# The opening in another order with transfers held back, and the recurrence's norm with low parts by GpSimd and its last sums in PSUM

## The chip, the cores and the metric

The kernel runs on one core of one Trainium2 chip. The metric is the device time of one execution in microseconds (us), the median of the runs. Engines: TensorE (PE in the rows, PEld its weight loads), VectorE (DVE), ScalarE (ACT), GpSimd (POOL), SyncE (SP), whose queue issues all transfers.

## The reference

Two transformer-like blocks over 512 tokens of width 1024, in float32. What bears on the change:

```python
def first_block(x, mem, ...):
    n = rmsnorm(h, norm_mix_pre)
    proj = n @ w_in                     # pool input, q k v, memory queries xq, gates
    y_pool = pool_mixer(p_in, w_pool_mix, pool_scale) @ w_pool_o   # trailing means over 2, 4, 8, 16 tokens
    y_sb = stick_breaking_attention(q, k, v) @ w_sb_o
    mem_n = rmsnorm(mem, norm_mem)      # 256 memory tokens
    y_x = memory_cross_attention(xq, mem_n, w_mem_kv) @ w_x_o      # 4 heads, softmax over 256
    ...
    ff = (silu(gu[..., :D_FF]) * gu[..., D_FF:]) @ w_ffn_out
    h = h + rmsnorm(ff, norm_ffn_post)

def second_block(x, ...):
    h = _rmsnorm(x, norm_mix[0])
    q, f, i, g = split(h @ hgrn_w_in, 4)
    o = chunk_gated_recurrence(silu(q), 1 - forget, i, log(forget))  # 8 heads of 128
    ...                                 # feed-forward, latent attention, feed-forward
```

## The kernel before

**Layout.** Activations lie feature by feature: a tile is 128 features by 512 tokens, eight tiles (KD = 8) make the residual; the memory's tiles are 128 by 256. Matrix products are float32 in three parts: weight and operand are each split into a high part (ScalarE copies them into a float32r buffer) and a low part (value less high part), and `products` (L220) issues high x high, low x high and high x low, lines 226 to 228. A norm's gain is applied with the high and low parts of its input (L426 or L1200 on ScalarE, L309 or L1240 on VectorE); its 1/rms is applied to the product's output (`dve_scaled`, L367), so the products of a norm start before its sum of squares is known.

**Weights.** All weights pass through one stream of units: a unit is eight 128 x 128 blocks (512 KB), and there are four slots (SLOTS). SyncE loads unit u into slot u % 4 once the low part of unit u - 4 is done (`s_lo`); ScalarE makes its high part (`high`, L201) once TensorE has used unit u - 4; GpSimd makes its low part in two halves of 512 columns (L2709, L2710), except units 0 to 6 and two later ones, which VectorE does (L465, L1275). `high_to(u)` places ScalarE's high parts in its program. Every engine runs its own program in order; the order is written out by hand, and an engine waits at a semaphore with everything behind it.

**Opening** (`act_start`, `dve_start`, `pe_memory`). Units 0 to 3 are the memory's keys and values: TensorE multiplies each with the eight memory tiles, 24 matmuls of 256 columns a unit. ScalarE's order is: high part of unit 0, memory tiles 0 to 3, unit 1, memory tiles 4 to 7, units 2 to 4, input tiles 0 and 1, unit 5, input tiles 2 and 3, unit 6, squares of the memory, input tiles 4 to 7, their squares. VectorE's order follows it. SyncE's order is: first gains, unit 0, the memory in two halves, units 1 to 3, input tiles 0 and 1, unit 4, tiles 2 and 3, units 5 and 6, tiles 4 to 7, the remaining parameters (1.6 MB), positions, unit 7. Then `pe_norm_start` takes units 4 to 6 together (WIDE = 3): for each of the eight input tiles nine matmuls of 512 columns.

**Memory values and cross-attention** (`pe_memory_values`, `pe_cross`, `dve_cross`). The values are transposed in two steps of two transposes, both through the same bank, each followed by a copy by ScalarE (L508). Then, for each of four token blocks tb: scores of four heads (L591), VectorE's maxima (L702), ScalarE's exponentials (L664), VectorE's probabilities (L713), and TensorE's transposes of them (L612). TensorE puts a weight tile of 24 matmuls (the next pool group or the first stick query) between scores and transposes; VectorE works on a pool group (`dve_pool`: copies L565, shifted sums L566, L569, L572) between the probabilities of one block and the maxima of the next.

**Recurrence's norm** (`dve_last_kept`, `act_post_norm`, `dve_post_norm`, stage "hgrn"). Before it VectorE finishes the feed-forward's output and its squares' sum in two halves of the tokens (L1157), each followed by a sum over partitions on TensorE and rstd on ScalarE; the low part of the norm's third unit stands between the two half sums. Then per tile j: VectorE scales and adds to the residual (L1217, L1220), ScalarE makes the high part (L1200), VectorE the low part (L1240), TensorE nine matmuls. Tile 0 goes in two halves. The squares go through two buffers, VectorE adds the seven sums at the end (L324), and TensorE forms the total over partitions (L280, one float32 matmul, which stands as two instructions in the trace) in the middle of the tile g of the first head. After the total come ScalarE's rstd (L285, L287) and the first head's chain.

## Time and profile before

| | |
|---|---|
| three runs, median | 2038.65 us (2036.48 to 2039.67) |
| the profiled execution, time | 2039.15 us |
| its span, first to last instruction | 2037.3 us |
| instructions | 26328 |
| VectorE, ScalarE, GpSimd busy | 47%, 45%, 42% |
| chain that ended last, TensorE's share | 91% |
| mean granted TensorE clock | 0.994 |

The span is 1.85 us shorter than the execution's own time; the rest lies outside the first and last instruction. In the views a row gives the start (us from the span's start), the duration, engine, line, operation, output and inputs, and in brackets how long the engine had been idle before and who released it. The duration of a matmul reaches over its pipeline; the pace of a row of matmuls is read from their starts.

### The profile page before, as it was taken

What the parts mean: (1) busy time and instruction counts of PE and PEld (TensorE: products, weight loads), DVE (VectorE), ACT (ScalarE), POOL (GpSimd) and SP (SyncE); (2) the same over time, 40 slices, a digit from 0 to 9 for tenths busy, and PEclk for the clock granted to TensorE, in tenths of its full rate; (3) what the DMA queues carried; (4) which work ended last, traced back from release to release, by engine and by line L of the source; (5) the groups of instructions that cost most, each with busy time, mean ns of one, the idle gap of its engine ahead of it and who ended that gap; (6) DMA issues with size and microseconds to landing.
All of it is one profiled execution on the core that took longest, in us unless ns stands there. A gap on an engine that the chain in (4) does not pass through costs nothing.

```text
span 2037.3 us, 26328 instructions
## 1 busy us (share of the span) xinstructions
PE 1996.1 (98%) x10819; PEld 1616.2 (79%) x10819; DVE 956.6 (47%) x1475; ACT 924.6 (45%) x1286; POOL 851.4 (42%) x668
## 2 busy tenths in 40 slices
PE   7999999999999998899999999999999999999999
PEld 6788888878888887677777888888876778888887
DVE  5744433254301315888885453155155555521551
ACT  6566554343313324665665443244266545432441
POOL 1243344535544552333435444444431254444442
PEclk9999999999999999899999999999999999999999
DMA  6122222223322322121212232232210222332321
GB/s 246 52 91 75 73 83 83 90 76 106 101 93 97 100 94 72 53 74 64 74 64 83 93 104 93 84 113 93 88 47 26 79 85 91 104 102 84 103 96 71
DMA packets 51672, 178.30 MB, mean 88 GB/s; under 512 B 5728, under 2 KB 8928, under 8 KB 51424
## 3 DMA queue, kind: packets, MB, share of 16 engines
...
q14 instruction: 34, 0.28, 0.0%
...
## 4 chain that ended last, share of the span: by engine, by line
PE 91%; DVE 5%; ACT 2%; issue 1%; POOL 1%; DMA 0%; SPq 0%; ACTq 0%; DVEq 0%; POOLq 0%
PE ps_gemm L226 24%; PE ps_gemm L228 23%; PE ps_gemm L227 23%; PE ps_attend L226 4%; PE ps_attend L227 4%; PE ps_attend L228 4%; PE ps_attend L1671 1%; PE ps_attend L838 1%; PE ps_attend L2457 1%; PE ps_attend L2523 1%; PE ps_attend L2458 1%; PE ps_attend L280 1%; ACT weights_high L201 1%; PE ps_gemm L1651 1%; PE ps_attend L1700 0%
## 5 line engine op out<-in xcount | busy, mean ns | idle before, releaser
L2709 POOL TENSOR_TENSOR weights_low<-weights_raw,weights_high 128x512 fp32r<-128x512 f32 (+1 forms) x332 | 426.0, 1283 | 1164.5 <-ACT weights_high L201 1164.1
L226 PE MATMUL ps_gemm<-normed_high,weights_high 128*128 128x512 f32 x1665 | 663.3, 398 | 6.0 <-DVE normed_low L1240 2.8
L228 PE MATMUL ps_gemm<-normed_low,weights_high 128*128 128x512 f32 x1665 | 648.5, 390 | 0.0
L227 PE MATMUL ps_gemm<-normed_high,weights_low 128*128 128x512 f32 x1665 | 648.3, 389 | 0.0
L201 ACT ACTIVATE weights_high<-weights_raw 128x1024 fp32r<-128x1024 f32 (+1 forms) x341 | 340.7, 1006 | 450.3 <-PE ps_attend L228 218.8
L2710 POOL TENSOR_TENSOR weights_low<-weights_raw,weights_high 128x512 fp32r<-128x512 f32 (+1 forms) x332 | 440.7, 1327 | 0.0
L226 PEld LDWEIGHTS ps_gemm<-normed_high,weights_high 128*128 128x128 f32 x1665 | 314.0, 189 | 79.3 <-issue 8.6
L227 PEld LDWEIGHTS ps_gemm<-normed_high,weights_low 128*128 128x128 f32 x1665 | 314.3, 189 | 65.2 <-issue 3.6
L228 PEld LDWEIGHTS ps_gemm<-normed_low,weights_high 128*128 128x128 f32 x1665 | 313.8, 188 | 65.7
L226 PE MATMUL ps_gemm<-operands_high_low,weights_high 128*128 128x512 f32 (+1 forms) x552 | 216.1, 391 | 0.9 <-POOL weights_low L2710 0.5
L228 PE MATMUL ps_gemm<-operands_high_low,weights_high 128*128 128x512 f32 (+1 forms) x552 | 214.2, 388 | 0.0
L227 PE MATMUL ps_gemm<-operands_high_low,weights_low 128*128 128x512 f32 (+1 forms) x552 | 214.1, 388 | 0.0
L367 DVE TENSOR_TENSOR scratch<-ps_gemm,rstd 128x512 f32<-128x512 f32 x89 | 60.8, 688 | 217.4 <-PE ps_gemm L228 200.5
L367 DVE TENSOR_TENSOR squares<-ps_gemm,rstd 128x512 f32<-128x512 f32 x106 | 73.0, 689 | 161.9 <-PE ps_gemm L228 130.1
L1401 ACT ACTIVATE ps_attend<-squares,parameters 128x512 f32<-128x512 f32 x88 | 68.9, 783 | 170.2 <-DVE squares L367 170.1
L226 PE MATMUL ps_attend<-operands_high_low,weights_high 128*128 128x512 f32 (+1 forms) x336 | 128.8, 383 | 10.3 <-DVE operands_high_low L309 10.2
L227 PE MATMUL ps_attend<-operands_high_low,weights_low 128*128 128x512 f32 (+1 forms) x336 | 127.8, 380 | 0.0
L228 PE MATMUL ps_attend<-operands_high_low,weights_high 128*128 128x512 f32 (+1 forms) x336 | 127.7, 380 | 0.0
L226 PEld LDWEIGHTS ps_gemm<-operands_high_low,weights_high 128*128 128x128 f32 x552 | 103.7, 188 | 23.0 <-issue 1.6
L228 PEld LDWEIGHTS ps_gemm<-operands_high_low,weights_high 128*128 128x128 f32 x552 | 103.6, 188 | 21.4
L227 PEld LDWEIGHTS ps_gemm<-operands_high_low,weights_low 128*128 128x128 f32 x552 | 103.7, 188 | 21.0 <-issue 0.2
L1461 DVE SCALAR_TENSOR_TENSOR ps_attend<-squares,parameters,ps_attend 128x511 f32<-128x511 f32 x88 | 66.4, 755 | 76.0 <-ACT ps_attend L1401 76.0
...
## 6 DMA issues: line engine op xcount, KB each, us to landing
...
```

The lines of the kernel that those rows point to most:

```text
L201: s.op.activation(m.wh[:, j * UNIT:j * UNIT + w], m.raw[:, j * UNIT:j * UNIT + w], ACT.Copy).then_inc(m.s_hi, 1)
L226: t.op.matmul(out, m.wh[:, c:c + P], xh, start=start and n == 0, stop=False, skip_group_check=True)
L227: t.op.matmul(out, m.wl[:, c:c + P], xh, start=False, stop=False, skip_group_check=True)
L228: ins = t.op.matmul(out, m.wh[:, c:c + P], xl, start=False, stop=stop and n == len(pairs) - 1, skip_group_check=True)
L280: t.op.matmul(out, m.col("ones", 0, P), src, start=True, stop=True).then_inc(*m.T.mark(*event))
L367: return v.op.tensor_tensor(dst, ps, m.rstd[:, 0:dst.shape[1]], ALU.mult)
L838: ins = t.op.matmul(zb[:, o:o + S - j * P], neg_tri if j == kb else neg_ones, x[:, ZOFF[j]:ZOFF[j] + S - j * P], start=False, stop=False, ...
L1401: s.op.activation(y, m.sq_tile(half), ACT.Identity, bias=m.col(f"conv_b{n - 1}", c), scale=m.col(f"conv_w{n - 1}", 88 + c)).then_inc(*m.A. ...
L1461: v.op.scalar_tensor_tensor(out=y[:, 1:S], in0=u[:, 0:S - 1], scalar=w(1), in1=y[:, 1:S], op0=ALU.mult, op1=ALU.add).then_inc(*m.V.mark(st ...
L1651: ins = t.op.matmul(bank[:, (c + 1) * P:(c + 1) * P + b - a], x.vtok[:, c * P:(c + 1) * P], x.cross[:, a:b], start=False, stop=c == 2, ski ...
L2709: g.op.tensor_tensor(m.wl[:, a], m.raw[:, a], m.wh[:, a].bitcast(F32), ALU.subtract)
L2710: g.op.tensor_tensor(m.wl[:, b], m.raw[:, b], m.wh[:, b].bitcast(F32), ALU.subtract).then_inc(m.s_lo, 1)
```

## The change

It has four parts.
- Opening. Unit 0's high and low parts are made in two halves, with memory tile 0 between them; all memory tiles come before unit 1; units 5 and 6 stand together. The memory is transferred in three parts (tiles 0 and 1, 2 and 3, 4 to 7). SyncE waits for unit 0 to have landed before it issues unit 2. Input tiles 2 and 3 go out behind unit 6, 4 and 5 behind unit 7, 6 and 7 behind unit 8; the remaining parameters and the positions behind unit 9.
- Memory values and cross-attention. The four transposes of the values go out together, with one copy. Half a weight tile stands ahead of the first scores, and each further half ahead of the next scores; VectorE's maxima stand inside the pool group, after its first sum; the low part of one pool group moves.
- The second half sum ahead of the recurrence is placed before the low part of a unit.
- Recurrence's norm. For tiles 4 to 7 ScalarE makes a scaled float32 copy beside the high part, and GpSimd subtracts, before its low part of the norm's fourth unit. ScalarE squares every tile right behind its high part, each into a place of its own. VectorE adds five of the sums; TensorE adds the squares of tiles 6 and 7 in PSUM in the sum over partitions, straight behind the norm.

```diff
--- before.py
+++ after.py
@@ -247,6 +249,9 @@
+GPSIMD_LOWS, VECTOR_SUMS = 4, 5
...
 def pieces(stage):
@@ -330,19 +335,42 @@
+def low_done(m, stage, j, half):
...
+    return (m.G if stage == "hgrn" and j >= GPSIMD_LOWS else m.V).at(*piece_event(stage, "low", j, half))
...
 def pe_norm_start(m, t, stage, events):
...
     for kb, half in pieces(stage):
-        t.wait_ge(*m.V.at(*piece_event(stage, "low", kb, half)))
+        t.wait_ge(*low_done(m, stage, kb, half))
...
             pe_memory_total(m, t)
-    if stage not in ("ffn0", "hgrn"):
+    if stage == "hgrn":
+        pe_total_of_squares(m, t, stage)
+    elif stage != "ffn0":
         pe_norm_total(m, t, stage)
...
+def square_place(m, j):
...
+    return (m.ss[:, :], m.sq_tile(1), m.sq_tile(0))[j] if j < 3 else m.big_tile(j)
...
+def pe_total_of_squares(m, t, stage):
...
+    for j in range(VECTOR_SUMS + 1, KD):
+        t.wait_ge(*m.A.at(stage, "square", j))
+        t.op.matmul(m.ab(3), m.col("ones", 0, P), square_place(m, j), start=j == VECTOR_SUMS + 1, stop=False,
+                    skip_group_check=True)
+    t.wait_ge(*m.V.at(stage, "sum", VECTOR_SUMS))
+    t.op.matmul(m.ab(3), m.col("ones", 0, P), m.ss[:, :], start=False, stop=True, skip_group_check=True)\
+        .then_inc(*m.T.mark(stage, "total"))
 def pe_norm_total(m, t, stage):
@@ -378,6 +406,13 @@
+MEMORY_PARTS = ((0, 2), (2, 4), (4, 8))
+def memory_part(j):
+    return [a <= j < b for a, b in MEMORY_PARTS].index(True)
@@ -387,8 +422,12 @@
 def pe_memory(m, t):
...
     for j in range(4):
-        base = take_unit(m, t)
+        base = take_unit(m, t) if j else 0
         for kb in range(KD):
+            if j == 0:
+                t.wait_ge(*m.V.at("first", "low"))
+                if kb == KD // 2:
+                    take_unit(m, t)
@@ -422,7 +461,7 @@
             (src, hi, _), gain = start_tile(m, stage, j)
-            s.wait_ge(*((m.s_x[j // 2], 16) if stage == "in" else (m.s_mem[j // 4], 16)))
+            s.wait_ge(*((m.s_x[j // 2], 16) if stage == "in" else (m.s_mem[memory_part(j)], 16)))
@@ -433,16 +472,21 @@
     s.tables(LOGEXP)
-    high_to(m, s, 0)
-    s.wait_ge(m.s_gains, 16)
-    highs("mem", range(4))
-    high_to(m, s, 1)
-    highs("mem", range(4, KD))
+    s.wait_ge(m.s_raw[0], 16)
+    for half in range(2):
+        sl = slice(half * UNIT // 2, (half + 1) * UNIT // 2)
+        ins = s.op.activation(m.wh[:, sl], m.raw[:, sl], ACT.Copy)
+        if half == 0:
+            ins.then_inc(*m.A.mark("first", "high"))
+            s.wait_ge(m.s_gains, 16)
+            highs("mem", range(1))
+    ins.then_inc(m.s_hi, 1)
+    s.unit += 1
+    highs("mem", range(1, KD))
...
     highs("in", (0, 1))
-    high_to(m, s, 5)
+    high_to(m, s, 6)
     highs("in", (2, 3))
-    high_to(m, s, 6)
@@ -472,15 +516,18 @@
-    weights((0,))
-    lows("mem", range(4))
-    weights((1,))
-    lows("mem", range(4, KD))
-    weights((2, 3, 4))
+    sl = slice(0, UNIT // 2)
+    v.wait_ge(*m.A.at("first", "high"))
+    v.op.tensor_tensor(m.wl[:, sl], m.raw[:, sl], m.wh[:, sl].bitcast(F32), ALU.subtract).then_inc(*m.V.mark("first", "low"))
+    lows("mem", range(1))
+    sl = slice(UNIT // 2, UNIT)
+    v.wait_ge(m.s_hi, 1)
+    v.op.tensor_tensor(m.wl[:, sl], m.raw[:, sl], m.wh[:, sl].bitcast(F32), ALU.subtract).then_inc(m.s_lo, 1)
+    lows("mem", range(1, KD))
+    weights((1, 2, 3, 4))
     lows("in", (0, 1))
-    weights((5,))
+    weights((5, 6))
     lows("in", (2, 3))
-    weights((6,))
@@ -495,17 +542,13 @@
 def pe_memory_values(m, t):
-    for j in range(2):
-        t.wait_ge(*m.V.at("mem", "kv", 2 + j))
-        if j:
-            t.wait_ge(*m.A.at("mem", "values", j - 1))
-        pe_to_tokens(m, t, ("mem", "values", j), m.ab(2), m.big[:, (2 + j) * M:(3 + j) * M], 2)
+    t.wait_ge(*m.V.at("mem", "kv", 3))
+    pe_to_tokens(m, t, ("mem", "values"), m.ab(2), m.big[:, 2 * M:4 * M], 4)
 def act_memory_values(m, s):
-    for j in range(2):
-        s.wait_ge(*m.T.at("mem", "values", j))
-        s.op.activation(m.big[:, (4 + j) * M:(5 + j) * M], m.ab(2, M), ACT.Copy).then_inc(*m.A.mark("mem", "values", j))
+    s.wait_ge(*m.T.at("mem", "values"))
+    s.op.activation(m.big[:, 4 * M:6 * M], m.ab(2), ACT.Copy).then_inc(*m.A.mark("mem", "values"))
@@ -549,7 +592,7 @@
-def dve_pool(m, v, g):
+def dve_pool(m, v, g, between):
@@ -564,6 +607,8 @@
         v.op.tensor_tensor(dst[:, w:S], src[:, w:S], src[:, 0:S - w], ALU.add).then_inc(*m.V.mark("pool", "sum", g, k))
+        if k == 0:
+            between()
@@ -580,9 +625,15 @@
 def pe_cross(m, t):
     keys, vals, xq, prob, pt = cross_tiles(m)
-    t.wait_ge(m.s_par, 16)
-    t.wait_ge(*m.V.at("cross", "q", 1))
-    t.wait_ge(*m.V.at("mem", "kv", 3))
+    def tile(tb, half):
+        bank = pool_bank(tb + 1)
+        if half == 0 and bank < 2:
+            t.wait_ge(*m.V.at("cross", "q", bank))
+        if half == 0 and tb == TB - 1:
+            t.wait_ge(*m.A.at("pool", "scaled", 0))
+        event = ("pool", tb + 1) if tb < TB - 1 else ("stick", "q", 0)
+        pe_tile(m, t, event, m.gb(bank), m.nh, m.nl, (2 * half, 2 * half + 1))
@@ -592,27 +643,26 @@
+    tile(0, 0)
+    t.wait_ge(m.s_par, 16)
+    t.wait_ge(*m.V.at("cross", "q", 1))
...
     for tb in range(TB):
-        bank = pool_bank(tb + 1)
-        if bank < 2:
-            t.wait_ge(*m.V.at("cross", "q", bank))
-        if tb == TB - 1:
-            t.wait_ge(*m.A.at("pool", "scaled", 0))
-        event = ("pool", tb + 1) if tb < TB - 1 else ("stick", "q", 0)
-        pe_tile(m, t, event, m.gb(bank), m.nh, m.nl, (0, 1))
+        tile(tb, 1)
...
             pe_pool(m, t, tb - 1)
-        pe_tile(m, t, event, m.gb(bank), m.nh, m.nl, (2, 3))
         if tb < TB - 1:
+            tile(tb + 1, 0)
             scores(tb + 1)
+        else:
+            t.wait_ge(*m.A.at("pool", "scaled", 1))
+            pe_tile(m, t, ("stick", "k", 0), m.gb(3), m.nh, m.nl, (0,))
         t.wait_ge(*m.V.at("cross", "prob", tb))
-        t.wait_ge(*(m.A.at("cross", "pt", tb - 1) if tb else m.A.at("mem", "values", 1)))
+        t.wait_ge(*(m.A.at("cross", "pt", tb - 1) if tb else m.A.at("mem", "values")))
...
         ins.then_inc(*m.T.mark("cross", "pt", tb))
-    t.wait_ge(*m.A.at("pool", "scaled", 1))
-    pe_tile(m, t, ("stick", "k", 0), m.gb(3), m.nh, m.nl, (0, 1))
+    pe_tile(m, t, ("stick", "k", 0), m.gb(3), m.nh, m.nl, (1,))
@@ -698,6 +748,8 @@
     def maxima(tb):
+        if tb == TB:
+            return
@@ -713,10 +765,10 @@
         ins.then_inc(*m.V.mark("cross", "prob", tb))
-        dve_pool(m, v, tb)
-        if tb < TB - 1:
-            maxima(tb + 1)
-        if tb:
+        if tb == TB - 1:
+            dve_pool_low(m, v, TB - 3)
+        dve_pool(m, v, tb, lambda: maxima(tb + 1))
+        if tb and tb != TB - 2:
@@ -1201,12 +1253,18 @@
             act_half_rstd(m, s, before, 1)
-        if half != (0,) and j < 3:
+        if stage == "hgrn" and j >= GPSIMD_LOWS:
+            s.op.activation(scaled_tile(m, j), src, ACT.Identity, scale=m.col(gain, j))\
+                .then_inc(*m.A.mark(stage, "scaled", j))
+        if stage == "hgrn" and half != (0,):
+            s.op.activation(square_place(m, j), src, ACT.Square).then_inc(*m.A.mark(stage, "square", j))
+        elif half != (0,) and j < 3:
...
             high_to(m, s, late)
-    for j in range(3, KD):
-        act_square(m, s, stage, j, residual_tile(m, j)[0])
+    if stage == "ffn0":
+        for j in range(3, KD):
+            act_square(m, s, stage, j, residual_tile(m, j)[0])
 def dve_branch(m, v, before, stage, j, half, post_gain):
@@ -1235,6 +1293,8 @@
     def low(j, half):
+        if stage == "hgrn" and j >= GPSIMD_LOWS:
+            return
@@ -1254,8 +1314,15 @@
         dve_unit_low(m, v, fourth_unit(m, stage))
-    for j in range(1, KD):
-        dve_square_sum(m, v, stage, j)
+    if stage == "hgrn":
+        for j in range(1, VECTOR_SUMS + 1):
+            v.wait_ge(*m.A.at(stage, "square", j))
+            if j > 1:
+                v.wait_ge(*m.V.at(stage, "sum", j - 1))
+            v.op.tensor_tensor(m.ss[:, :], m.ss[:, :], square_place(m, j), ALU.add).then_inc(*m.V.mark(stage, "sum", j))
+    else:
+        for j in range(1, KD):
+            dve_square_sum(m, v, stage, j)
 def fourth_unit(m, stage):
@@ -1502,8 +1569,8 @@
             dve_half_sum(m, v, "ffn0out", 0)
+    dve_half_sum(m, v, "ffn0out", 1)
     dve_unit_low(m, v, fourth_unit(m, "hgrn") - 1)
-    dve_half_sum(m, v, "ffn0out", 1)
 def pe_post_ffn(m, t):
@@ -1726,9 +1793,7 @@
     else:
-        g_tile((0, 1))
-        pe_norm_total(m, t, "hgrn")
-        g_tile((2, 3))
+        g_tile(range(4))
@@ -2695,6 +2760,19 @@
+def scaled_tile(m, j):
...
+    return m.big_tile(4 + j)
...
+def gpsimd_lows(m, g, stage):
...
+    for j in range(GPSIMD_LOWS, KD):
+        _, hi, lo = residual_tile(m, j)
+        g.wait_ge(*m.A.at(stage, "scaled", j))
+        g.op.tensor_tensor(lo, scaled_tile(m, j), hi.bitcast(F32), ALU.subtract).then_inc(*m.G.mark(stage, "low", j))
...
 def gpsimd_program(m, g):
@@ -2703,6 +2781,8 @@
             continue
+        if u == fourth_unit(m, "hgrn"):
+            gpsimd_lows(m, g, "hgrn")
@@ -2711,7 +2791,7 @@
-INPUT_BEHIND = {3: (0,), 4: (1,), 6: (2, 3)}
+INPUT_BEHIND = {3: (0,), 6: (1,), 7: (2,), 8: (3,)}
 def sync_program(m, q):
@@ -2723,16 +2803,18 @@
             q.wait_ge(m.s_lo, u - SLOTS + 1)
+        elif u == 2:
+            q.wait_ge(m.s_raw[0], 16)
...
         if u == 0:
-            for k in range(2):
-                sl = slice(k * 4 * M, (k + 1) * 4 * M)
+            for k, (a, b) in enumerate(MEMORY_PARTS):
+                sl = slice(a * M, b * M)
...
                 q.op.dma_start(m.h[:, sl], m.dram_x[:, sl]).then_inc(m.s_x[k], 16)
-        if u == SLOTS + WIDE - 1:
+        if u == SLOTS + WIDE + 2:
```

## Rows read from the trace of the kernel before

**Rows 1.** Page, section 1: busy time and share of the span, TensorE to GpSimd

```profile
PE 1996.1 (98%) x10819; PEld 1616.2 (79%) x10819; DVE 956.6 (47%) x1475; ACT 924.6 (45%) x1286; POOL 851.4 (42%) x668
```

**Rows 2.** Waits, TensorE, whole span: engine line, released by, us in total, times, longest

```profile
PE ps_attend L226 <- DVE operands_high_low L309: 10.2, 2, 8.2
...
PE ps_gemm L1648 <- DVE scratch L1948: 3.6, 1, 3.6
...
PE ps_gemm L280 <- DVE sum_of_squares L1157: 2.8, 2, 1.6
```

**Rows 3.** Timeline of TensorE in the opening (columns as told above)

```profile
8.16 0.55 PE L226 MATMUL ps_attend<-operands_high_low,weights_high 128*128 128x256 f32 x1 [8.16 <-DVE operands_high_low L309]
...
13.10 0.58 PE L226 MATMUL ps_attend<-operands_high_low,weights_high 128*128 128x256 f32 x1 [2.04 <-DVE operands_high_low L309]
...
17.01 0.28 PE L226 MATMUL ps_attend<-operands_high_low,weights_high 128*128 128x256 f32 x1
...
24.92 0.40 PE L226 MATMUL ps_gemm<-normed_high,weights_high 128*128 128x512 f32 x1
```

**Rows 4.** Timeline of ScalarE and VectorE in the opening

```profile
4.57 1.06 ACT L201 ACTIVATE weights_high<-weights_raw 128x1024 fp32r<-128x1024 f32 x1 [2.56 <-DMA weights_raw<-weights_full]
...
6.99 1.71 ACT L426 ACTIVATE operands_high_low<-scratch,parameters 128x256 fp32r<-128x256 f32 x4 [1.36 <-DMA scratch<-memory_tiles]
...
7.53 1.68 DVE L309 SCALAR_TENSOR_TENSOR operands_high_low<-scratch,parameters,operands_high_low 128x256 fp32r<-128x256 f32 x4 [0.65 <-ACT operands_high_low L426]
...
10.34 1.06 ACT L201 ACTIVATE weights_high<-weights_raw 128x1024 fp32r<-128x1024 f32 x1 [1.64 <-DMA weights_raw<-weights_full]
...
23.40 1.23 DVE L465 TENSOR_TENSOR weights_low<-weights_raw,weights_high 128x1024 fp32r<-128x1024 f32 x1 [0.33 <-ACT weights_high L201]
```

**Rows 5.** Windows (busy us by engine, clock, DMA share, GB/s); landing of weights_raw, 0 to 60

```profile
10.00:20.00 10.00, 7.96 (x48) 7.67 (x48) 7.63 (x10) 7.41 (x11) 0.00 (x0) 1.00 0.95 369
...
48.00:50.00 2.00, 2.00 (x7) 1.51 (x6) 1.75 (x2) 0.00 (x0) 2.00 (x2) 0.50 0.66 190
...
DMA to landing us min/median/max: 3.2/7.7/11.8
```

**Rows 6.** Timeline of TensorE from the memory's values to the kept product

```profile
46.48 0.41 PE L374 MATMUL ps_attend<-parameters,scratch 128*128 128x128 f32 x2 [3.47 <-ACT scratch L508]
...
48.69 0.63 PE L227 MATMUL ps_gemm<-normed_high,weights_low 128*128 128x512 f32 x1
...
91.70 1.02 PE L531 MATMUL ps_gemm<-sum_of_squares,parameters 128*128 128x512 f32 x2
```

**Rows 7.** Timeline of VectorE at the end of cross-attention

```profile
83.80 1.14 DVE L565 COPY sum_of_squares<-squares 128x2 f32<-128x2 f32 x1
...
90.47 1.28 DVE L723 TENSOR_TENSOR operands_high_low<-ps_attend,operands_high_low 128x512 fp32r<-128x512 f32 x2
```

**Rows 8.** Timeline of TensorE at the recurrence's norm

```profile
798.99 0.55 PE L226 MATMUL ps_gemm<-normed_high,weights_high 128*128 128x256 f32 x1 [2.43 <-issue]
...
807.78 0.50 PE L226 MATMUL ps_gemm<-normed_high,weights_high 128*128 128x512 f32 x1 [0.62 <-DVE normed_low L1240]
...
820.93 1.02 PE L280 MATMUL ps_attend<-sum_of_squares,parameters 128*128 128x512 f32 x2
```

**Rows 9.** Timeline of GpSimd, ScalarE and VectorE at the recurrence's norm and behind it

```profile
805.89 1.29 POOL L2710 TENSOR_TENSOR weights_low<-weights_raw,weights_high 128x512 fp32r<-128x512 f32 x1
...
806.08 1.65 DVE L1240 SCALAR_TENSOR_TENSOR normed_low<-residual,parameters,normed_high 128x512 fp32r<-128x512 f32 x1
...
806.20 0.72 ACT L1200 ACTIVATE normed_high<-residual,parameters 128x512 fp32r<-128x512 f32 x1 [1.30 <-DVE residual L1220]
...
814.69 5.39 DVE L324 TENSOR_TENSOR sum_of_squares<-sum_of_squares,squares 128x512 f32<-128x512 f32 x7
...
823.38 1.89 DVE L367 TENSOR_TENSOR scratch<-ps_gemm,rstd 128x512 f32<-128x512 f32 x3 [3.30 <-ACT rstd L287]
...
836.23 3.60 POOL L2709 TENSOR_TENSOR weights_low<-weights_raw,weights_high 128x512 fp32r<-128x512 f32 x1 [9.31 <-ACT weights_high L201]
```

6 lines of the change are left out of this document (4 added, 2 removed).

## The prediction

> **What bounds the kernel now.** I read the page first: TensorE is busy 98% of the span [rows 1], so a wait is worth removing only where TensorE itself stands still. The waits of TensorE over the whole span [rows 2] therefore come next. They are few, and they lie in the three places that the diff touches: the opening (10.2 us until the memory's low parts), the memory's values (3.5 us), and the start of the recurrence (3.6 us, and 2.8 us at the two half totals ahead of it). Last I read the timelines of those three places. What to see in them:
>
> Opening. TensorE starts at 8.16, stops after 12 matmuls, and starts again at 13.10 [rows 3]. The cause is one line up in ScalarE's list: memory tiles 4 to 7 stand behind the high part of the second unit, which waited for its transfer until 10.34 [rows 4]. From 13.10 to 17.01 there are 18 matmuls of 256 columns (0.22 us each, the lower clock level), from 17.01 to 24.92 there are 66 (0.12 us each, the upper level). The 96 matmuls of the memory product need 11.5 us at the upper level and now end at 24.92. The DMA engines move 369 GB/s in the stretch 10 to 20, with a share of 0.95, so transfers are a second limit close by [rows 5].
>
> Memory values. TensorE waits 3.47 us for a copy by ScalarE; behind it the granted clock is 0.50 of full, 1.2 GHz [rows 5], and six 512-column matmuls go at 0.43 us instead of 0.23 (one of them in [rows 6]).
>
> Recurrence. From the norm's total on the chain is ScalarE's rstd, then VectorE from 823.38, and it ends in TensorE's wait for VectorE of 3.6 us [rows 2, 9]. TensorE is not the bound there; the time of rstd is.
>
> The sum is made against the profiled execution, span 2037.3 and time 2039.15; the median of the three runs is 0.5 us below that.
>
> **Part 1, the opening.** Unit 0 is split in two, and only one memory tile stands between its halves. Unit 0 still lands at about 4.5: fewer transfers are outstanding, but the bytes ahead of it are the same. A half high part is half of 1.06, 0.55 us; a tile's high part is 1.71/4 = 0.43; a half low part 0.6, a tile's low part 0.42 [rows 4]. So: half high 5.1, half low 5.75, tile high 5.6, tile low 6.2. TensorE starts at 6.3 to 6.8 instead of 8.16. Tiles 1 to 7 follow at 0.42 us each on VectorE (6.9 to 10.1), faster than TensorE's six half-pace matmuls per two tiles (0.64 us a tile), so unit 0 ends near 11.4. The second unit is no longer ahead of tiles 4 to 7: high part 9.7 to 10.75, low part until 12.0 (1.23 [rows 4]). If the clock is up by then, three units at 2.88 us end at 20.7. Then the first norm needs unit 6. Its transfer goes out when unit 2's low part is done (13.2), behind unit 5. Bytes issued up to and with unit 6 are 5.4 MB; at 369 GB/s from 2 on [rows 5] they are in at 16.7 when served in order, but transfers share the engines, and the median landing in this stretch is 7.7 us after issue [rows 5]: 17 to 21, I take 19. High part 1.05 and low part 1.23 put the start of the norm at 21.2. Gain 24.92 - 21.2 = 3.7 us. Ends: 5 us if nothing is late and the clock rises by 10; 1.5 us if unit 6 takes the longest landing seen (11.8 us, to 25, is excluded only by its having less behind it, so I take 21.5 plus high, low and a TensorE still at the low level for 2 us). The inputs x (now behind units 3, 6, 7, 8) I cost at nothing: the first pair keeps its place, and tiles 4 to 7 are wanted only after eight microseconds of norm matmuls. The late parameters and positions go out three units later, about 17.5 to 19.5 instead of 16.7; they are wanted past 40, so that is free, and they leave the DMA to units 7 to 9.
>
> **Part 2, values and cross-attention.** The two copies become one, and half a tile (12 matmuls, 2.73 us) is put ahead of the scores, so the copy and the scaled queries are hidden. On today's clock: the first two transposes end at 43.0 (46.48 less the wait), the other two 0.3 later, the half tile at 46.0 and the scores (1.06) at 47.1, all at the upper level. That removes 3.5 us of waiting and 1.2 + 0.2 us of slow matmuls. From there VectorE decides. Its reduction of the scores is now placed after the first sum of each pool group, in order, so what is queued behind it (the rest of the pool group, then the next probabilities) waits for TensorE, where the scores come half a tile later. Played through with today's durations VectorE waits about 1.8 and 1.3 us there, and ends the fourth pool group at 86.3 and the attention's low parts at 88.3; those low parts today start at 90.47 and end 91.75 [rows 7]. TensorE starts the kept product, which needs them, at 88.4 instead of 92.6 [rows 6]. Gain 4.2; I take 3.7 because small VectorE copies that meet a GpSimd low part take 1.14 us instead of 0.15 [rows 7], and which of them meet one I can't tell. Ends 1.5 and 5.
>
> **Part 3, the recurrence's norm.** (a) The second half sum goes ahead of VectorE's low part of a unit (1.23 us): total and rstd of the second half come 0.9 us earlier, the first half's branch 0.7 us later, TensorE starts at 798.2 instead of 798.99 [rows 8]: 0.8 us. The wait of 0.62 before 807.78 [rows 8] goes with it: it is VectorE's low part of 1.65 us, which met GpSimd's [rows 9]. (b) VectorE drops four low parts of 0.7 us and two of seven sums (5.39/7 = 0.77 each [rows 9]); its sums begin at 814.7 - 2.6 (the lows) - 0.9 (the stall) - 0.5 (the earlier rstd) = 810.7. ScalarE has three passes per tile in place of two, each at most the 0.72 of a high part [rows 9], about 2.0 us, against TensorE's nine matmuls at 0.228, 2.06 us. GpSimd's low of 512 columns is 1.29 [rows 9]. The three are matched; the last low part comes at 814.5, so the norm ends at about 816.8 instead of 818.2 (820.93 less half a tile, 2.73). (c) TensorE gets three float32 sums in place of one: each is a pair of instructions and 0.86 us, +1.72 us, ahead of the total. (d) The low part of the unit after the norm is queued behind GpSimd's four: until 818.6. It is wanted at 820, so it is covered by a hair; uncovered it would cost 1 to 2 us of TensorE, which has room there. (e) VectorE's five sums, each with both operands in SBUF, now run beside GpSimd's last two lows and two weight halves. The row of 806.08 shows VectorE waiting for GpSimd's end [rows 9]; alternating, four of the sums wait 1.3 us each, and the fifth ends at 810.7 + 5 x 0.7 + 4 x 1.3 = 819.4. So the total is done at 820.2 against 821.8 (820.93 + 0.86 [rows 8]): 1.6 us. Without (e) TensorE alone would set it, 816.8 + 3 x 0.86 = 819.4, a gain of 2.4.
>
> The Trainium skill (SBUF — State Buffer, section "Who interferes with whom") states the rule that speaks against this part: a VectorE instruction with two SBUF inputs and a GpSimd instruction that reads SBUF exclude each other, whichever starts first. The row of 1.65 us agrees; without that rule part 3 would be 2.4, by it 1.6.
>
> rstd moves VectorE's chain (823.38) by the same amount, and TensorE's own work behind it (two tiles, 10.9 us) still fits. I take 1.6, ends 0 and 3.
>
> **Sum.** 3.7 + 3.7 + 1.6 = 9.0 us; 2039.15 - 9.0 = 2030.1, which I leave at 2030.0 against the median. Between these places TensorE waits for nobody longer than about a microsecond [rows 2], so what one of them gives is not taken back in the next.
>
> **Rivals.**
> 1. Only TensorE's side moves, VectorE's does not: in cross-attention its in-order wait for the later scores costs 2.7 us three times, less the 1.5 us it no longer waits; part 2 gives about 1.5 and unit 6 is late, part 1 gives 2: total 5 with part 3, 2034.3. For it: 0.95 DMA share, and VectorE at the end of that stage just in time. Against it: VectorE has some 7 us of waiting in that stage to absorb it.
> 2. The change doesn't do what it says in the opening: transfers share the engines so evenly that holding back unit 2 changes nothing, TensorE again stops before unit 1, and stays at the low level. Part 1 then gives 0.5 and the rest 5.3: 2033.4; with part 2 at its low end as well, 2036.
> 3. Slower: the exclusion of (e), at its dearest. One GpSimd half took 3.60 us at 836.23 [rows 9]. If each of VectorE's five sums waits for such a one, the fifth ends at 810.7 + 5 x (0.7 + 3.6) = 832, rstd is 11 us late, and TensorE, out of work, falls to the lower level for another 1.5 us: 2039.15 - 7.4 + 11 + 1.5 = 2044.2. Part 3 turns into a loss from a GpSimd instruction of 1.7 us on, and the whole kernel is slower from about 3 us on. Against it: the usual one is 1.3, and only six are near.
> 4. All goes through: 5 + 5 + 3, 2026.
>
> **How the numbers follow.** Forecast and its surroundings (2027.5 to 2032.5) 0.60; rival 4: 0.10; rivals 1 and 2 (2032.5 to 2036.5) 0.24; rival 3: 0.06 (not all of it past the bound). Range 2026.0 to 2035.5, which leaves 0.03 below and about 0.13 above. A measurement of this kernel tells 0.2%, 4.1 us, from no change: faster is below 2034.6, so 0.83; same 0.12; slower 0.05.
>
> **What would show it.** Right: the first norm matmul near 21 and no stop of TensorE before it longer than 1 us; no wait at the values' transposes and 512-column matmuls at 0.23 us behind them; the kept product about 8 us earlier than today; VectorE's last sum near 819 less 7.4, with sums of 2 us where GpSimd is busy; TensorE's wait for VectorE after the first head still about 3.5. Wrong: unit 6's transfer landing past 22, VectorE idle over 5 us for scores, or TensorE waiting for GpSimd's lows for more than 1 us in the norm.

## The result, and the profile after

The changed kernel takes 2026.64 us (median of 4 runs, 2025.69 to 2027.85) against 2038.91 (4 runs, 2036.48 to 2039.67): ratio 0.9938, 95% interval 0.9926 to 0.9950, a gain of 12.3 us where 9.0 was forecast. The two profiled executions differ by 12.5 us in span (2037.3 and 2024.8). Read at the same events, 11.8 us of the gain arise in the three places and nothing between them, and 0.7 us behind the last of them:

| event | before, us | after, us | lead | gained in the stretch |
|---|---|---|---|---|
| first TensorE matmul | 8.16 | 7.11 | 1.05 | 1.05 |
| first matmul of the first norm | 24.92 | 21.66 | 3.26 | 2.21 |
| fourth pool product (cross-attention) | 91.70 | 82.66 | 9.04 | 5.78 |
| last half tile of the feed-forward's branch | 791.89 | 782.92 | 8.97 | -0.07 |
| first matmul of the recurrence's norm | 798.99 | 789.03 | 9.96 | 0.99 |
| VectorE starts behind rstd | 823.38 | 811.55 | 11.83 | 1.87 |
| end of the span | 2037.3 | 2024.8 | 12.5 | 0.7 |

TensorE's waits over the whole span after the change (engine, line, released by; total, times, longest) answer to [rows 2]:

```profile
PE ps_attend L228 <- DVE operands_high_low L314: 7.1, 1, 7.1
PE ps_gemm L228 <- DVE normed_low L1300: 4.7, 4, 2.5
PE ps_attend L1738 <- DVE squares L2001: 2.5, 1, 2.5
PE ps_gemm L1715 <- DVE scratch L2013: 2.2, 1, 2.2
PE ps_gemm L285 <- DVE sum_of_squares L1209: 2.2, 2, 1.6
...
PE ps_gemm L228 <- POOL weights_low L2790: 1.0, 3, 0.5
```

The wait at the values is gone, the opening has one start in place of two, and GpSimd's low parts of the norm appear nowhere as a releaser. TensorE in the opening, to be read against [rows 3] (the row of 21.34 is the last of the memory's 96 matmuls):

```profile
7.11 0.55 PE L228 MATMUL ps_attend<-operands_high_low,weights_high 128*128 128x256 f32 x1 [7.11 <-DVE operands_high_low L314]
...
11.45 0.28 PE L228 MATMUL ps_attend<-operands_high_low,weights_high 128*128 128x256 f32 x1
...
12.76 0.36 PE L228 MATMUL ps_attend<-operands_high_low,weights_high 128*128 128x256 f32 x1 [0.43 <-DVE weights_low L509]
...
21.34 0.28 PE L230 MATMUL ps_attend<-operands_high_low,weights_high 128*128 128x256 f32 x1
...
21.66 0.47 PE L228 MATMUL ps_gemm<-normed_high,weights_high 128*128 128x512 f32 x1
```

From the start to 11.3 the pace is 0.21 us a matmul, from 11.45 on 0.12. I read this as the lower level (1.2 GHz) and the upper (2.4 GHz). The views' own figure for the granted clock reads 1.00 in both stretches, so in the opening the level is known from the pace alone; it is the same halving as that of the 512-column matmuls, 0.43 against 0.23 us, where the views do show 0.50 (48 to 50 in [rows 5]). Before, the slow pace lasted until 16.9 with a stop of 2.04 us inside. ScalarE and VectorE feed it:

```profile
4.68 0.63 ACT L478 ACTIVATE weights_high<-weights_raw 128x512 fp32r<-128x512 f32 x1 [2.67 <-DMA weights_raw<-weights_full]
5.94 0.51 ACT L465 ACTIVATE operands_high_low<-scratch,parameters 128x256 fp32r<-128x256 f32 x1 [0.63 <-DMA scratch<-memory_tiles]
...
10.31 1.99 ACT L203 ACTIVATE weights_high<-weights_raw 128x1024 fp32r<-128x1024 f32 x2
...
19.19 1.06 ACT L203 ACTIVATE weights_high<-weights_raw 128x1024 fp32r<-128x1024 f32 x1 [0.93 <-DMA weights_raw<-weights_full]
```

```profile
20.28 1.23 DVE L509 TENSOR_TENSOR weights_low<-weights_raw,weights_high 128x1024 fp32r<-128x1024 f32 x1 [0.48 <-ACT weights_high L203]
```

Unit 6 is there at 19.2 and its low part ends at 21.51; the norm starts 0.15 us behind that. TensorE's own row of matmuls ends at 21.46 (the last start and 0.12 us of pace). So two limits now meet within 0.05 us, the transfer of unit 6 and TensorE's 96 matmuls: an earlier transfer alone would give at most 0.2 us. In cross-attention, TensorE in the changed kernel (busy time of TensorE, its weight loads, VectorE, ScalarE and GpSimd, then granted clock, DMA share and GB/s), and below it the second wait of the kernel before, which [rows 2] doesn't show:

```profile
22.00:82.00 60.00, 59.87 (x284) 44.40 (x283) 45.39 (x90) 36.63 (x80) 22.68 (x16) 1.00 0.35 131
```

```profile
PE ps_attend L612 <- DVE scratch L713: 0.8, 1, 0.8
```

TensorE waits nowhere in this stage after the change, apart from 0.13 us at 71.44, and the granted clock stays at 1.00. Before, it waited 3.5 and 0.8 us, and for 3.4 us (47.6 to 51.0) the clock stood at 0.50, which costs half of that, 1.7 us. Together that is 6.0 us, and the stretch is 5.8 shorter: 61.0 us is TensorE's own work, and TensorE is the limit of the stage. VectorE there:

```profile
50.60 1.23 DVE L754 TENSOR_REDUCE small<-ps_attend 128x4 f32<-128x1024 f32 x1
...
59.09 1.23 DVE L754 TENSOR_REDUCE small<-ps_attend 128x4 f32<-128x1024 f32 x1 [1.30 <-PE ps_attend L642]
60.34 0.17 DVE L757 TENSOR_SCALAR small<-small 128x4 f32<-128x4 f32 x1
60.42 0.16 DVE L608 COPY sum_of_squares<-squares 128x2 f32<-128x2 f32 x1
...
74.99 1.15 DVE L608 COPY sum_of_squares<-squares 128x2 f32<-128x2 f32 x1
...
81.68 1.28 DVE L775 TENSOR_TENSOR operands_high_low<-ps_attend,operands_high_low 128x512 fp32r<-128x512 f32 x2
```

Inside the pool groups VectorE waits for the scores 1.3 us twice (59.09 and 67.57), and not at all the first time. The copy of two columns takes 0.16 us at 60.42 and 1.15 at 74.99, where it meets a GpSimd low part (74.37 to 76.11). The attention's low parts end at 82.96, 0.16 us before the first matmul of the kept product (83.12), so VectorE is close to being the limit but isn't. In the recurrence's norm, VectorE, GpSimd and TensorE:

```profile
800.96 2.39 DVE L1322 TENSOR_TENSOR sum_of_squares<-sum_of_squares,squares 128x512 f32<-128x512 f32 x2
803.46 4.99 DVE L1322 TENSOR_TENSOR sum_of_squares<-sum_of_squares,scratch 128x512 f32<-128x512 f32 x3
811.55 1.89 DVE L395 TENSOR_TENSOR scratch<-ps_gemm,rstd 128x512 f32<-128x512 f32 x3 [3.11 <-ACT rstd L292]
```

```profile
803.21 1.30 POOL L2773 TENSOR_TENSOR normed_low<-scratch,normed_high 128x512 fp32r<-128x512 f32 x1 [0.41 <-ACT scratch L1257]
804.47 1.73 POOL L2789 TENSOR_TENSOR weights_low<-weights_raw,weights_high 128x512 fp32r<-128x512 f32 x1
806.16 1.73 POOL L2790 TENSOR_TENSOR weights_low<-weights_raw,weights_high 128x512 fp32r<-128x512 f32 x1
```

```profile
789.03 0.55 PE L228 MATMUL ps_gemm<-normed_high,weights_high 128*128 128x256 f32 x1 [2.46 <-DVE normed_low L1300]
...
807.39 1.88 PE L369 MATMUL ps_attend<-scratch,parameters 128*128 128x512 f32 x4
809.11 1.02 PE L372 MATMUL ps_attend<-sum_of_squares,parameters 128*128 128x512 f32 x2
...
846.28 1.13 PE L1715 MATMUL ps_gemm<-scratch 128*128 128x128 f32 x8 [2.23 <-DVE scratch L2013]
```

VectorE's fifth sum ends at 808.5, 0.7 us before TensorE asks for it: TensorE goes from the norm through its three float32 sums without a wait.

### The profile page after: what moved, and what is told of

Read it like the earlier page. It is cut to its first block, busy times and chain, and to the rows that moved or that the text cites. A ratio compares the mean times of both kernels' runs of the same rounds, so it can differ in the third digit from the quotient of the medians.

```text
span 2024.8 us, 26338 instructions
## 1 busy us (share of the span) xinstructions
PE 1992.9 (98%) x10823; PEld 1613.2 (80%) x10823; DVE 953.5 (47%) x1470; ACT 927.1 (46%) x1290; POOL 859.0 (42%) x672
## 4 chain that ended last, share of the span: by engine, by line
PE 93%; DVE 4%; ACT 2%; issue 1%; POOL 1%; DMA 0%; SPq 0%; DVEq 0%; ACTq 0%; POOLq 0%
PE ps_gemm L228 24%; PE ps_gemm L230 24%; PE ps_gemm L229 24%; PE ps_attend L228 4%; PE ps_attend L230 4%; PE ps_attend L229 4%; PE ps_attend L1738 1%; PE ps_attend L890 1%; PE ps_attend L2522 1%; PE ps_attend L2588 1%; PE ps_attend L2523 1%; PE ps_attend L285 1%; PE ps_gemm L1718 0%; PE ps_attend L1767 0%; PE ps_attend L903 0%
## 6 DMA issues: line engine op xcount, KB each, us to landing
scratch<-positions SPq DMA_DIRECT2D x1, 256.0 KB, 11.8
```

## The experiments

All kernels compute the whole reference. For each, the stretches between the events of the table say more than the time alone: the opening (start of the first norm), cross-attention (from there to the fourth pool product), and the norm (last half tile of the feed-forward's branch to VectorE behind rstd). Before they are 24.92, 66.78 and 31.49 us; after 21.66, 61.00 and 28.63. The stretch between cross-attention and the feed-forward's end was 700.2 to 700.3 us in all of them.

A stretch is one reading of one execution. Seven of the kernels, the changed one included, have the same instructions in the norm, and its stretch is 28.6 to 29.2 us in them, 28.9 in the mean. What differs is mostly the granted clock, which is at 0.50 when the norm starts and stays there for 3.2 to 5.3 us: 4.0 us in the changed kernel, 5.3 with unit 0 whole, whose stretch is 0.6 longer. The norms below are held against the 28.9. Where two kernels' times differ by about 1 us, their intervals overlap, and the stretches carry the argument.

| kernel | time, us | ratio to before, 95% | opening | cross | norm |
|---|---|---|---|---|---|
| opening alone | 2036.86 | 0.9983 to 1.0001 | 22.54 | 66.81 | 31.58 |
| cross alone | 2032.11 | 0.9956 to 0.9980 | 25.23 | 60.94 | 31.54 |
| norm alone | 2034.80 | 0.9972 to 0.9990 | 23.83 | 66.85 | 29.02 |
| nothing held back | 2026.88 | 0.9929 to 0.9954 | 21.31 | 61.00 | 28.69 |
| unit 0 whole | 2028.18 | 0.9933 to 0.9960 | 21.67 | 61.02 | 29.21 |
| unit 1 between tiles | 2030.72 | 0.9951 to 0.9976 | 25.34 | 60.94 | 28.68 |
| maxima behind the group | 2032.43 | 0.9956 to 0.9981 | 22.29 | 65.40 | 28.94 |
| maxima inside, old TensorE order | 2033.63 | 0.9967 to 0.9986 | 21.98 | 67.71 | 29.13 |
| six sums | 2028.58 | 0.9939 to 0.9964 | 22.06 | 60.91 | 30.15 |
| three sums | 2029.36 | 0.9942 to 0.9969 | 22.32 | 61.02 | 30.73 |
| lows on VectorE | 2028.29 | 0.9938 to 0.9963 | 21.99 | 60.96 | 29.55 |
| first low early | 2028.78 | 0.9935 to 0.9960 | 22.33 | 61.04 | 29.37 |

**Each part alone.** The kernel before with one part of the change:

```diff
# opening alone: the order of units and tiles, the transfers
-    high_to(m, s, 1)
+    highs("mem", range(1, KD))
-INPUT_BEHIND = {3: (0,), 4: (1,), 6: (2, 3)}
+INPUT_BEHIND = {3: (0,), 6: (1,), 7: (2,), 8: (3,)}
# cross alone: pe_memory_values, act_memory_values, pe_cross, dve_pool and its maxima
# norm alone: the half sum, GpSimd's lows, the squares, five sums, TensorE's sums
```

> The kernel before with the opening's part of the change alone (ScalarE's, VectorE's and SyncE's order, memory in three parts, unit 2 held back). Theory A, the parts add up as the two traces stand to each other: the first norm matmul at 21.7 instead of 24.9, all that follows 3.3 us earlier, the wait for the values' copy and the slow matmuls behind it unchanged, 2038.9 - 3.3 = 2035.6 us. Theory B, the opening is tied to the cross-attention (its late parameters and inputs meet the old order): under 1.5 us, 2037.5 or more.

> The kernel before with the part on memory values and cross-attention alone. Theory A: the fourth pool group's product 5.8 us earlier than before (91.7 to 85.9), 2033.1 us. Theory B, 3.7 us as predicted is what this part gives by itself and the rest came from its meeting with the opening: 2035.2 us.

> The kernel before with the recurrence's norm alone, the second half sum moved ahead included. Theory A: first matmul of the norm 1.0 us earlier, rstd 2.85 us earlier, and 0.7 us more at the first head, where the matmuls behind TensorE's wait run at the upper clock level: 2038.9 - 3.4 = 2035.5. Rival (the predicted 1.6 us was right and the rest is another effect): 2037.3.

Against 2038.35 us the gains are 1.5, 6.2 and 3.6 us, 11.3 together, and 12.3 for the whole change. The opening's time lies between its two theories, the other two are near or past theory A. The stretches are cleaner. Cross-attention gives 5.8 us with the old opening and with the new; the norm gives 31.5 - 29.0 = 2.5 alone and 2.9 in the changed kernel, which the scatter above covers. So the parts add up; none needs another. The opening is the noisy one: with the old opening the first norm started at 24.92, 25.23 and 23.83, with the new one at 22.54 here. Most of this scatter is the moment at which TensorE's pace changes. In the ten profiles whose first row of matmuls has no stop of over a microsecond inside the slow pace, it changes 3.6 to 6.5 us behind the first matmul: 4.3 us in the changed kernel, and 6.5 here, with the same opening. The landings add to it; the first matmul starts between 7.1 and 8.0. So from one pair of profiles 3.26 can't be told from 2.5, and the time of the opening alone (interval up to 1.0001) isn't separated from no change.

**The opening.** First the held-back transfer, then the split of unit 0, then the place of unit 1:

```diff
# nothing held back
-        elif u == 2:
-            q.wait_ge(m.s_raw[0], 16)
```

> The changed kernel without SyncE's wait for unit 0 ahead of unit 2; nothing else. Theory A, the reordering of ScalarE's and VectorE's work makes the gain and holding transfers back gives little: unit 0 and the first memory tiles land within 0.5 us of the changed kernel, the first norm matmul at 21.7 to 22.2, 2026.6 to 2027.1. Theory B, the held transfers are the gain: unit 1 lands past 10 as before, TensorE stops ahead of it for over 1.5 us, 2028.5 or more.

```diff
# unit 0 whole
+    high_to(m, s, 0)
+    s.wait_ge(m.s_gains, 16)
+    highs("mem", range(KD))
# unit 1 between tiles: as unit 0 whole, and
-    highs("mem", range(KD))
+    highs("mem", range(4))
+    high_to(m, s, 1)
+    highs("mem", range(4, KD))
```

> The changed kernel with weight unit 0 converted whole, ahead of all memory tiles, as before the change; everything else as changed. Theory A (the split buys TensorE its early start, and the chain through the four first products passes it on): first TensorE matmul at about 8.1 us in place of 7.1, first norm matmul at 22.4 to 22.7, time 0.7 to 1 us over the changed kernel's, about 2027.5. Theory B (the norm's start hangs on ScalarE and VectorE finishing unit 6, whose order does not change, so the early start is lost in waits): first norm matmul stays at 21.3 to 22.0 and the time within 0.3 us of the changed kernel's.

> The changed kernel with unit 0 whole and unit 1's conversion back ahead of memory tiles 4 to 7, as before the change; transfers, the order of the inputs and unit 6 ahead of unit 5's old place stay as changed. Splitting unit 0 and holding back transfers moved the first norm matmul by less than the scatter (21.3 to 22.5 in all kernels with the new opening, 23.8 to 25.2 with the old). Theory A (the place of unit 1 is the part that gains: TensorE stops after 12 matmuls until unit 1 has landed and been converted, and its clock rises later): a stop of 1 to 2.5 us near 10, first norm matmul at 23.5 to 24.5, time 1.5 to 2.5 us over the kernel with unit 0 whole, about 2030. Theory B (unit 6 and the order of the inputs are the part that gains): the stop is there but the norm starts at 21.5 to 22.5, and the time stays near 2028.

Without the hold nothing is lost: first norm at 21.31, no stop of TensorE, 2026.88 us. That is theory A, with the norm 0.4 us earlier than its range. With unit 0 whole TensorE starts 0.7 us later and the norm at the same 21.67: the start that the split buys is spent again before unit 1, where the changed kernel's TensorE waits 0.43 us for the low part (12.76). In both kernels TensorE's matmuls and the low part of unit 6 end at 21.5. (Its time, 2028.18, is 1.5 us above the changed kernel's, with an interval that overlaps; theory B gave 0.3. The stretches put 0.6 of it into the norm and none into the opening.) With unit 1 back between the tiles everything is back. TensorE in the kernel with unit 1 between the tiles, and behind it the change of pace with unit 0 whole:

```profile
7.97 0.55 PE L228 MATMUL ps_attend<-operands_high_low,weights_high 128*128 128x256 f32 x1 [7.97 <-DVE operands_high_low L314]
...
12.51 0.58 PE L228 MATMUL ps_attend<-operands_high_low,weights_high 128*128 128x256 f32 x1 [1.64 <-DVE operands_high_low L314]
...
18.63 0.28 PE L229 MATMUL ps_attend<-operands_high_low,weights_low 128*128 128x256 f32 x1
...
25.34 0.40 PE L228 MATMUL ps_gemm<-normed_high,weights_high 128*128 128x512 f32 x1
```

```profile
12.63 0.29 PE L229 MATMUL ps_attend<-operands_high_low,weights_low 128*128 128x256 f32 x1
```

The stop of 1.64 us is only half of the price. Behind it the matmuls go at 0.21 us until 18.6; with unit 0 whole they do so until 12.6. That is 8.8 us at the slow pace against 4.8, and half of the difference, 2.0 us, is lost on top of the stop: 3.7 in all, which is 25.34 - 21.67. This pair is a dear one. Over all profiles, the slow pace lasts 5.9 to 8.8 us (7.2 in the mean, without the stop) in the four that stop ahead of unit 1, and 3.6 to 6.5 (5.1) in the ten that don't, and the norm starts at 24.8 and 22.0 in the means: the stop and what follows it cost 2.8 us. The two times differ by 2.5 us. Of the opening's edits the place of unit 1 carries the gain, since the held transfer and the new order of the inputs and of unit 6 are all still in this kernel and don't save it, and undoing the hold or the split moved the norm's start by less than the scatter. The stop and the time are those of theory A; the norm's start, 25.34, is later than its 24.5. ScalarE waits for unit 1's transfer 1.42 us until 9.75 there, while tiles 4 to 7 could have been converted.

**Cross-attention.** The change moves TensorE's scores and values, and VectorE's maxima. Each undone:

```diff
# maxima behind the group
-        if k == 0:
-            between()
-        dve_pool(m, v, tb, lambda: maxima(tb + 1))
+        dve_pool(m, v, tb, None)
+        maxima(tb + 1)
# maxima inside, old TensorE order: pe_memory_values, act_memory_values and pe_cross as before
```

> The changed kernel with VectorE's maxima behind the whole pool group, where they stood before; TensorE's order stays the new one. Theory A, the maxima inside the pool group let ScalarE's exponentials run beside VectorE, and that is worth the 2 us of waiting per block that they removed: VectorE waits 2.0 us for exponentials in each of the four blocks again, and the fourth pool group ends late, TensorE waits at the probabilities or the pool product, 2 to 4 us in all, 2028.6 to 2030.6. Theory B, TensorE's new order alone makes the gain (VectorE had room): 2026.6 to 2027.2.

> The changed kernel, but TensorE's order in the cross attention and the transposes of the values are those of before; VectorE still takes its maxima inside the pool group. Theory (the two halves need each other: TensorE's stop of 3.47 us at the values and its clock fall come back, and by then VectorE's early maxima find scores that are early enough or not, but the gain of the pool group cannot be used in full): the stretch from the first norm matmul to the fourth pool product, 61.0 us in the changed kernel and 66.8 before, is 64 to 66 us, and the time lies 3 to 5 us over the changed kernel's, 2029.5 to 2031.5. Rival (the gain is VectorE's alone, TensorE's order adds only what it showed by itself, 1.4 us): the stretch is 62.4 and the time 2028.

With TensorE's order alone the stretch is 65.4 us, 1.4 less than before (the time, 2032.43, is above the range of theory A). With VectorE's order alone it is 67.7, worse than before (66.8), and outside both expectations (64 to 66, and 62.4). Together 61.0. With the maxima behind the group, VectorE, then TensorE's waits in this stage and a window with its granted clock (0.50, behind the five busy times):

```profile
55.45 0.18 DVE L760 RECIPROCAL small<-small 128x4 f32<-128x4 f32 x1 [2.00 <-ACT scratch L712]
...
59.24 1.12 DVE L608 COPY sum_of_squares<-squares 128x2 f32<-128x2 f32 x1
...
65.22 0.18 DVE L760 RECIPROCAL small<-small 128x4 f32<-128x4 f32 x1 [1.41 <-ACT scratch L712]
```

```profile
PE ps_attend L661 <- DVE scratch L763: 2.2, 1, 2.2
PE ps_gemm L574 <- DVE scratch L615: 0.6, 1, 0.6
```

```profile
78.60:82.00 3.40, 3.40 (x9) 1.49 (x9) 3.33 (x5) 2.12 (x3) 3.27 (x3) 0.50 0.12 25
```

With the maxima inside and TensorE's old order, TensorE's stop, the window behind it, and VectorE:

```profile
43.62 0.66 PE L402 MATMUL ps_attend<-parameters,scratch 128*128 128x128 f32 x2 [3.47 <-ACT scratch L555]
```

```profile
43.50:50.20 6.70, 6.58 (x19) 4.61 (x20) 1.80 (x4) 2.92 (x11) 3.78 (x4) 0.50 0.66 223
```

```profile
54.96 1.22 DVE L753 TENSOR_REDUCE small<-ps_attend 128x4 f32<-128x1024 f32 x1 [2.46 <-PE ps_attend L640]
```

Maxima behind the group: VectorE takes them last and then stands idle for ScalarE's exponentials, three times 2.0 us and once 1.4, and TensorE waits 2.2 us for the probabilities and 0.6 for a pool group. Behind the longer wait the granted clock falls to 0.50 for 3.4 us (78.6 to 82.0). The waits, 2.7, and half of the 3.4 make 4.4 us, which is 65.4 - 61.0. Maxima inside: the rest of the pool group fills VectorE's wait, and in the changed kernel 2.0 and 1.2 us are left of the four. So taking TensorE's stop at the values away alone uncovers another one, behind VectorE's chain, with another fall of the clock.

With TensorE's old order, VectorE stands 2.46 us in front of the scores, but TensorE waits only for the values' copy (3.47 us) and 0.14 us elsewhere; the 0.8 us for the probabilities are gone. What makes the stretch longer than before is the clock: it stays at 0.50 for 6.8 us behind the stop (43.5 to 50.3) in place of 3.4. Waits of 3.6 and half of 6.8 make 7.0, near the measured 67.7 - 61.0 = 6.7. Why the low level lasted twice as long isn't shown; with 3.4 us of it the sum would be 66, under the 66.8 of before. So the -0.9 of this half is the clock's, not the order's.

**The norm.** One number each:

```diff
-GPSIMD_LOWS, VECTOR_SUMS = 4, 5
+GPSIMD_LOWS, VECTOR_SUMS = 4, 6   # six sums; 4, 3: three sums; 8, 5: lows on VectorE
```

> The changed kernel with six sums on VectorE and one square less on TensorE. The theory that VectorE's sums and GpSimd's low parts exclude each other (1.7 us a sum where both work): VectorE's last sum ends 1.7 us later, at about 810.2, after TensorE is done with the other square (808.3), so the total comes at about 811.1, 1 us later than in the changed kernel, and the time is 1 us longer, 2027.6. Rival, no exclusion (0.77 us a sum): last sum 809.2, total at 810.1, no change of time.

> The changed kernel with the low parts of tiles 4 to 7 on VectorE again and no scaled copies; the squares, five sums on VectorE and three on TensorE stay. If GpSimd's low parts carry the gain of this part: VectorE is 2.6 us longer with the residual and each low part that meets GpSimd's weights waits 0.9, sums end past 811, total 2 to 3 us later, 2028.6 to 2029.6. If the squares and sums carry it: within 0.7 us of the changed kernel.

> The changed kernel with three sums on VectorE and two squares more on TensorE. TensorE then is the bound of the total: two float32 matmuls of 0.86 us more behind the norm, VectorE's sums end 3.4 us earlier without use; total 1.7 us later, 2028.3. Rival, VectorE's sums are what holds the total (TensorE waits for them): no change or faster.

TensorE with six sums, TensorE with three, and VectorE and TensorE with the low parts on VectorE:

```profile
810.81 1.12 PE L372 MATMUL ps_attend<-sum_of_squares,parameters 128*128 128x512 f32 x2 [1.70 <-DVE sum_of_squares L1322]
```

```profile
808.42 3.60 PE L369 MATMUL ps_attend<-scratch,parameters 128*128 128x512 f32 x8
```

```profile
804.97 1.41 DVE L1322 TENSOR_TENSOR sum_of_squares<-sum_of_squares,squares 128x512 f32<-128x512 f32 x2
806.42 2.15 DVE L1322 TENSOR_TENSOR sum_of_squares<-sum_of_squares,scratch 128x512 f32<-128x512 f32 x3
```

```profile
808.55 1.88 PE L369 MATMUL ps_attend<-scratch,parameters 128*128 128x512 f32 x4
810.27 1.02 PE L372 MATMUL ps_attend<-sum_of_squares,parameters 128*128 128x512 f32 x2
```

Six sums cost 1.3 us in the stretch against the mean of 28.9 (a sixth sum of 1.56 on VectorE, for which TensorE waits 1.70, less the pair of matmuls that it saves), three cost 1.8 (two more pairs of float32 matmuls, 1.72). Both go as their theories say in kind, with times 1 us above them. Five is where the two meet. With all low parts on VectorE five sums take 3.6 us, 0.7 each, as GpSimd is idle; in the changed kernel the first, which falls mostly between two low parts of GpSimd, takes 0.68, and the four others 1.6 to 1.7 each. The low parts on GpSimd more than double the price of those sums, and the last ends 19.3 to 19.4 us behind the norm's start either way. The gain of the low parts on GpSimd lies with TensorE, which reaches its own three sums 18.4 us behind the norm's start in place of 19.3. Of that 0.9 about 0.4 is the clock's, at 0.50 for 4.9 us in place of 4.0: the kernel with three sums has the 4.9 too, and TensorE gets there after 18.75. The other 0.5 us is what the low parts on GpSimd are worth. The stretch is thus near the second expectation (within 0.7 us); the time, 2028.29, lies between the two.

One neighbour was not tried. With the low parts on VectorE its fifth sum ends at 808.6, 1.7 us before TensorE asks for it at 810.27. A sixth would end at 809.3, and TensorE, with one pair less, would ask at 809.4. My estimate from these rows is 0.86 us less than the 29.55, 28.7 us: about what the changed kernel takes (28.6), without GpSimd's part.

**A try at a better kernel.** Nothing held back, and the first half tile's low part ahead of the second half's branch:

```diff
+            if stage == "hgrn" and n == 1:
+                low(*todo[0])
             dve_branch(m, v, before, stage, j, half, post_gain)
...
```

> The changed kernel without the held-back transfers, and at the recurrence's norm VectorE takes the low part of the first half tile ahead of the second half's branch (1.2 us of VectorE work that stood between). Theory: TensorE's wait for that low part, 2.46 us at 789.03, shrinks, but the second half's low part is then later by as much as VectorE's low part takes (0.35 us): the stretch from the end of the feed-forward to the first norm matmul falls from 6.1 to 5 to 5.5 us, the time to 2025.5 to 2026.5. Rival (TensorE then waits for the second half instead, and nothing of it reaches the end of the norm, which VectorE's sums set): the first norm matmul is early, the rstd comes at the same distance from the feed-forward's end, 28.6 us, and the time stays at 2026.7.

TensorE's wait is 2.40 us in place of 2.46 (2.59 without the hold alone): VectorE now waits 0.58 us for ScalarE's high part, which had been hidden under that branch, TensorE waits 0.33 us for the second half, and VectorE's sums begin 0.7 us later. The rival was right in that nothing reaches the end of the norm: its stretch is 29.37, no better than the 28.6 to 29.2 of the others. No version here beats the changed kernel.

## Why the prediction was right

**Opening, 3.7 forecast; 3.3 in the pair of profiles, 2.6 between the means (24.7 over three profiles with the old opening, 22.05 over nine with unit 1 behind the tiles and unit 0 split).** The steps hold nearly to the number in the pair: unit 6 in at 19.2 (19 forecast), the norm at 21.66 (21.2), the pace up at 11.45, unit 1's low part done at 12.6 (12.0), TensorE's matmuls through at 21.5 (20.7). TensorE's start was put too early, 6.3 to 6.8 against 7.1 to 8.0 in the profiles: tile 0's own transfer (0.63 us of ScalarE's wait at 5.94) was left out, and each half or single tile took 0.05 to 0.1 us more than its share of a longer row. It cost little, since TensorE waited for unit 1's low part at 12.76 all the same. The prediction had unit 6 as the only limit behind it; TensorE's own matmuls are the other. That the pace was up by 11.4 was luck in part: in the other profiles without a stop this happened at 11.0 to 14.4, which is part of the difference between 3.3 and 2.6. Rival 2 was right in half: holding back changes nothing. It was wrong that TensorE would then stop and stay cold, because the reordering alone prevents both.

**Values and cross-attention, 3.7 forecast, 5.8 measured.** The first step is right: the stop and the slow matmuls behind it go. The second, "From there VectorE decides", is wrong. TensorE is the limit of the stage: it stands 0.13 us in 61, and its waits and slow matmuls of before, 6.0 us, are the whole gain. The prediction had 4.9 of them in its terms (3.5 and 1.2 + 0.2), left out the second wait (0.8), and then let VectorE's chain take some away. That chain ended sooner than forecast. The waits for scores were 1.3 and 1.3 (1.8 and 1.3 forecast). The fourth pool group was put at 86.3 on the old clock and the low parts of the attention at 88.3; they came at 81.16 and 82.96, plus the opening's 3.26: 84.4 and 86.2. The mis-sized term in it is the small copies: I held all of today's collisions with GpSimd and took half a microsecond off for more. In the changed kernel three small instructions collide in the last group (74.99, 77.55, 79.30) and none at 60.42, 68.91 and 69.70, because the wait for scores moves the copies out of the GpSimd low part; with the maxima behind the group two of these, 59.24 and 68.99, cost 1.12 and 1.14 again. Rival 1 didn't come: VectorE's waits for the later scores are 0, 1.3 and 1.3 us, not three times 2.7. The kernel with the maxima behind the group gives 1.4, near that rival's 1.5, but by the wait for the exponentials.

**Norm, 1.6 forecast, 2.9 in the pair, 2.5 alone.** (a) holds: start at 789.03, on the old clock 798.0, forecast 798.2. (b) holds: the norm's matmuls end at 807.39, on the old clock 816.4 (816.8), with no wait for GpSimd. (c) holds: two pairs of float32 matmuls in 1.72 us. (d) holds: the next unit's two halves are done at 807.9 and wanted at 809.57. (e) is the one mis-sized. I priced four of the five sums at 2.0 us; they took 1.7 from start to start, 1.2 us less in all. The rule of the Trainium skill (SBUF — State Buffer, section "Who interferes with whom") shows in the trace in kind, with sums of 1.6 to 1.7 us against 0.7 with GpSimd idle; one strictly after the other would have given the 2.0, and the trace has less. The sums also began at 800.96, on the old clock 809.9, 0.8 us before the forecast 810.7. So the last ends at 808.5, on the old clock 817.4, not 819.4, and falls under TensorE's own end. The figure without (e), 2.4, was the one to take. Rival 3 had its condition (GpSimd instructions beside the sums) and not its price: they took 1.73, not 3.6.

**Behind the norm.** The prediction left the wait after the first head at 3.5; in the changed kernel it is 2.23. That in itself is worth nothing: in all fourteen profiles the wait ends 34.7 us behind rstd, whether it is 2.2 or 3.6 long, because VectorE's chain from rstd sets its end. The last 0.7 us of the gain are in the eight matmuls behind it, 1.13 us in place of 2.05. They fell into a stretch with the granted clock at 1.00, and before into one at 0.50 (the figure behind the five busy times; the changed kernel first):

```profile
846.30:847.50 1.20, 1.20 (x9) 1.14 (x10) 1.20 (x3) 0.00 (x0) 0.00 (x0) 1.00 0.89 328
```

```profile
858.20:860.00 1.80, 1.80 (x9) 1.80 (x10) 1.80 (x5) 0.00 (x0) 0.00 (x0) 0.50 0.70 273
```

This isn't the change's: the eight took 2.05 us in the kernel with unit 0 whole, which has the same instructions there, and 1.13 with the opening alone. What puts the low level there or elsewhere was not found.

The time lay inside the range, 0.6 us above its lower end, where rival 4 (all goes through, 2026, by 5 + 5 + 3) stood with a chance of 0.10. The three places and the kind of gain in each were right. In cross-attention the prediction had the wrong engine as the limit, and the two prices that were too high, the copies and the sums, were both collisions between VectorE and GpSimd that I let fall near their worst. The opening erred the other way by 1.1 us, held against the means, so part of the closeness is errors that offset each other. Two slips change nothing: rival 1's terms give 2034.1 and not 2034.3, and outside the three places TensorE waited up to 2.1 us in the kernel before (at 833.3), not about one.
